# Four turned-input buffers moved to directly behind the weight ring

## The reference

```python
h = x + short_conv_mixer(rms_norm(x), w_in, conv_w, w_out)     # 1024 -> 3072 -> 1024
h = h + swiglu_ffn(rms_norm(h), w13, w2)                       # 1024 -> 2 x 2816 -> 1024
h = h + mla_mixer(rms_norm(h), ...)                            # latent attention, 8 heads
h = h + swiglu_ffn(rms_norm(h), w13, w2)
h = rms_norm(h)
h = h + concat(gla_group(...), gqa_group(...)) @ w_out         # linear attention and attention
h = h + hier_moe(rms_norm(h), ...)                             # 64 experts, 2 per token, 1024 -> 512 -> 1024
return rms_norm(h)
```

## Time and profile before

| | before |
|---|---|
| median of 3 runs | 1616.76 us |
| profiled execution: from first to last instruction | 1615.7 us |
| PE busy (share of the span) | 1312.8 us (81%) |
| DVE busy | 538.6 us (33%) |
| ACT busy | 444.6 us (28%) |
| POOL busy | 63.0 us (4%) |
| moved by DMA | 519.44 MB, mean 321 GB/s |
| chain that ended last | DMA 49%, PE 46%, DVE 2%, ACT 2% |
| mean granted TensorE clock | 0.937 |

### The profile page before, as it was taken

The page is one execution under the profiler, slowest core; times in us unless marked ns, Lnnn a source line. Parts: engine busy times, 40 slices in busy tenths (PEclk is TensorE's granted clock), DMA queues, the critical chain, the costliest instruction groups (busy, mean ns, idle before and its releaser), DMA issues.

```text
span 1615.7 us, 29952 instructions
## 1 busy us (share of the span) xinstructions
PE 1312.8 (81%) x12872; PEld 989.5 (61%) x12872; DVE 538.6 (33%) x911; ACT 444.6 (28%) x760; POOL 63.0 (4%) x84
## 2 busy tenths in 40 slices
PE   8999999999999999999676667667666766666665
PEld 8989999878999989876343343344333334333332
DVE  6665555775555568641100000001001010010001
ACT  5444343654434356621111011011011011011101
POOL 3000000002000016000000000000000000000000
PEclk9999999999999999999888898799899889898888
DMA  9555544444554535499999999999999999999997
GB/s 357 191 172 184 191 171 154 144 159 144 183 187 175 196 131 223 190 416 428 424 428 428 428 428 429 429 428 428 428 428 428 428 428 428 428 429 429 428 429 300
DMA packets 46215, 519.44 MB, mean 321 GB/s; under 512 B 5583, under 2 KB 5844, under 8 KB 8660
## 3 DMA queue, kind: packets, MB, share of 16 engines
q1 hardware_dynamic: 44928, 517.38, 78.8%
q0 software_dynamic: 896, 0.99, 0.3%
q10 hardware_dynamic: 340, 0.35, 0.1%
HBM read 517.65 MB, written 1.05 MB: 321 GB/s over the span
## 4 chain that ended last, share of the span: by engine, by line
DMA 49%; PE 46%; DVE 2%; ACT 2%; issue 1%; SPq 0%; POOL 0%; ACTq 0%; POOLq 0%; DVEq 0%
DMA work<-in_moe_units 48%; PE ps L298 12%; PE ps L300 12%; PE ps L299 12%; PE ps L2233 5%; PE ps L2224 1%; PE ps L971 1%; PE ps L970 0%; ACT w_split L257 0%; PE ps L465 0%; DVE xT_lo L545 0%; PE ps L1672 0%; DMA work<-in_conv_w 0%; PE ps L2267 0%; PE ps L1654 0%
## 5 line engine op out<-in xcount | busy, mean ns | idle before, releaser
L2224 PE MATMUL ps<-ring,work 128*32 128x256 f32 x2976 | 203.8, 420 | 98.0 <-DMA ring<-in_moe_units 97.0
L298 PE MATMUL ps<-xT_hi,w_split 128*128 128x256 f32 x960 | 269.5, 281 | 1.4 <-DVE xT_lo L545 1.4
L299 PE MATMUL ps<-xT_lo,w_split 128*128 128x256 f32 x960 | 268.1, 279 | 0.0
L300 PE MATMUL ps<-xT_hi,w_split 128*128 128x256 f32 x960 | 267.9, 279 | 0.0
L2444 DVE TENSOR_TENSOR work<-ps,work 128x128 f32<-128x128 f32 x64 | 18.7, 292 | 745.2 <-ACT work L2358 745.2
L261 DVE TENSOR_TENSOR w_split<-ring,w_split 128x2048 fp32r<-128x2048 f32 (+3 forms) x101 | 225.4, 2234 | 96.2 <-ACT w_split L257 95.0
L257 ACT ACTIVATE w_split<-ring 128x2048 fp32r<-128x2048 f32 (+3 forms) x105 | 196.0, 1869 | 152.9 <-PE ps L300 152.9
L2224 PEld LDWEIGHTS ps<-ring,work 128*32 128x32 f32 x2976 | 95.6, 118 | 195.6 <-DMA ring<-in_moe_units 120.9
L298 PEld LDWEIGHTS ps<-xT_hi,w_split 128*128 128x128 f32 x960 | 180.2, 188 | 3.4 <-issue 2.2
L299 PEld LDWEIGHTS ps<-xT_lo,w_split 128*128 128x128 f32 x960 | 179.8, 187 | 1.0
L300 PEld LDWEIGHTS ps<-xT_hi,w_split 128*128 128x128 f32 x960 | 180.3, 188 | 0.0
(11 more groups left out here) (364 smaller groups left out, 1620.8 us busy)
## 6 DMA issues: line engine op xcount, KB each, us to landing
ring<-in_moe_units SPq DMA_DIRECT2D x124, 2048.0 KB, 27.0
ring<-in_ffn_units SPq DMA_DIRECT2D x66, 1024.0 KB, 4.8
x_slots<-in_moe_units SPq DMA_DIRECT2D x32, 2048.0 KB, 25.9
work<-in_moe_units SPq DMA_DIRECT2D x32, 2048.0 KB, 27.1
ring<-in_conv_units SPq DMA_DIRECT2D x15, 1024.0 KB, 12.0
ring<-in_win_units SPq DMA_DIRECT2D x9, 1024.0 KB, 5.0
ring<-in_wo_units SPq DMA_DIRECT2D x4, 1024.0 KB, 5.8
ring<-in_wout_units SPq DMA_DIRECT2D x4, 1024.0 KB, 4.8
```

What stands on the lines that cost most here:

```text
L298: pe.matmul(out_ap, stat_hi, mov_hi, start=first, stop=False, skip_group_check=True)
L299: pe.matmul(out_ap, stat_hi, mov_lo, start=False, stop=False, skip_group_check=True)
L300: return pe.matmul(out_ap, stat_lo, mov_hi, start=False, stop=last, skip_group_check=True)
L2224: last = pe.matmul(ps[CAP * j:CAP * j + CAP, b, 0:BLK], xstat[:, 4 * half + k, CAP * lane:CAP * lane + CAP], w[k][:, j // 2, BLK * (j % 2) ...
```

## The change

The declaration of `x_slots` moves up, from behind `h` to directly behind `ring`. Everything that names it stays as it is. The tensors `cst`, `wr`, `late_consts` (which lies over parts of these two), `pcol` and `h` are thereby placed 32,768 bytes higher, and `x_slots` lower.

```diff
         return ((U_MOE + 2) % RAW, (U_MOE + 4) % RAW, RAW + 2 * (U_WOUT % SPLIT), RAW + 2 * ((U_WOUT + 1) % SPLIT))[q]
 
+    x_slots = sb("x_slots", [P, 4, UNIT])
     cst = sb("cst", [P, NCONST])
     wr = sb("wr", [P, KD, NG + NE])
     behind = -(-(nc.lookup_mloc(cst).addr + 4 * CONST["causal"][0]) // 32) * 32
@@ -187,7 +188,6 @@
     late_consts = nc.alloc_sbuf_tensor_at("late_consts", [P, D], F32, offset=behind)
     pcol = sb("pcol", [P, NROWS])
     h = sb("h", [P, TT, D])
-    x_slots = sb("x_slots", [P, 4, UNIT])
     at = nc.lookup_mloc(x_slots).addr
     xT_hi, xT_lo, xS_hi, xS_lo = (nc.alloc_sbuf_tensor_at(name, [P, KD, T], F32R, offset=at + 4 * UNIT * q)
                                   for q, name in enumerate(("xT_hi", "xT_lo", "xS_hi", "xS_lo")))
```

## The result

The kernel with the change takes 1620.98 us (median of 13 runs, 1620.32 to 1622.15), the kernel before in the same session 1617.52 us (13 runs, 1616.63 to 1618.74). The ratio is 1.0022, 95% interval 1.0015 to 1.0030: 3.5 us slower, just past what can be told from no change. The forecast was no change, with 1614 to 1620 us as that case's own range: the time lies 1 us above this one, inside the wide range of 1612.0 to 1623.5, and in the window of the slower rival.

What follows compares the result with a forecast made beforehand. TensorE's pace was taken to bound the dense layers and weight transfers the experts; four terms of zero (0 + 0 + 0 + 0) left the median, 1616.8 us, with a range of 1612.0 to 1623.5 us.

Steps and rivals of the forecast that it cites:

- the slower rival: Dense layers' 256-column matmuls: both buffers on multiples of 128 bytes cost 1.1 to 2.2 ns each, +3.2 to +6.4 us; chance 0.10.
- Parts 1 to 3: Expert-weight loads into `x_slots`, expert matmuls reading it, VectorE and ScalarE on turned inputs: each zero; loads bounded at ±6.3 us.
- Part 4, "Against addresses": Dense split matmuls: two units with equal offsets modulo 16,384 differ in pace, so a pipeline phase fits better; zero taken.
- Part 4, "the 512-column matmuls don't care": Dense layers: similar durations, 392 ns with `zeros` and 394 with `w_split` and `xS`, so placement costs these nothing.
- Part 4, the count: Dense layers: 2,880 matmuls moving 256 columns of `xT` and 72 moving `xS`; zero, ends -12.9 and +6.4 us.
- The faster rival: Dense layers' 256-column matmuls drop to 113.3 ns at distance 0 modulo 16,384: -12.9 us, 1603.9 us; chance 0.13.
- The estimate of 109 ns: Split matmuls of 256 columns: N/2.4 + 2.5 ns from the skill's page, set against 117.7 and 113.3 in the trace.

Runs made afterwards that it cites:

- map_start: PE-only kernel on constant data: the same 48 matmuls of 256 columns at once behind 1 to 3 others; 113.3 or 117.8 ns at distances 64 and 192.
- near_192: Against the kernel before, `pcol` and `rounds_i`, then `x_slots`, stand directly behind the ring, distance 192 modulo 256: 1604.64 us, ratio 0.9921.
- parted: As near_192, but the turned inputs are parted: `xS` directly behind the ring at distance 0, `xT` at 192: 1611.73 us, ratio 0.9968 against before.
- map_pace: PE-only kernel, one source line for each matmul kind and distance; moving 256 input columns: 120.0, 117.8, 118.7, 113.3 ns at 0, 64, 128, 192.
- map_fine: PE-only kernel with the kinds of map_pace, distances in 16-byte steps, and both operands shifted together; group means from 114.2 to 120.0 ns between multiples of 64.

## Why the prediction failed where it did

The forecast of no change, on the ground that addresses don't set the pace, missed by 3.5 us against before. That the time still lies in the wide range is owed to the slower rival's window, which that range took in whole and which was given 0.10, and in part to luck: of the kinds of matmul that it left out or gave no cost at either end, one cost 2.1 us and the 512-column ones gave 4.1 back.

**Parts 1 to 3**, transfers into `x_slots`, expert matmuls, VectorE and ScalarE: zero was right. The period of the experts is 29.36 us, L808 takes 693 ns, the writes of ScalarE and VectorE into the turned inputs take as long as before, to within 0.15 us in the sum of every group, and the dense matmuls account for 4.4 of the shift of 4.5 us at the end of their stage.

**Part 4, "Against addresses"**, is the step that failed. The observation was sound: U_MLA+4 and U_MLA+8 had the same distance and different paces, and map_start shows that two paces at one distance can come from what ran before; for these two units themselves that isn't shown. What the prediction drew from it was not sound. "A phase fits better than a collision" treats the two as exclusive; the distance decides which phases exist, and at distance 0 neither 113.3 nor 117.8 does. The two paces at one address said nothing of what another address would bring.

**Part 4, "the 512-column matmuls don't care"**, failed too, and by the way it was read. It compared durations, and a pace of 0.26 us from a group of four with a slow first one, too coarse for a difference of 6.6 ns. The starts within one feed-forward unit give 233.3 ns, a number that the argument never looked at and that the `zeros` rows can't vouch for. It was worth -4.1 us (762 matmuls).

**Part 4, the count.** The 336 matmuls with `w_split` moving 256 columns past `xT` were not in the sum at all. They were at 113.8 ns and had the most to lose: +2.1 us.

**The slower rival** came true in its size for the term that it named: the 2,952 matmuls that move 256 columns of the inputs cost 6.11 + 0.31 = 6.4 us, its upper end. That the total is 3.5 and not 6.4 us comes from the two terms that it lacked, +2.1 and -4.1, and from scatter in the experts. Its mechanism, both buffers on multiples of 128, was half right: distance 0 stays at 120.0 when both are shifted off such a multiple, so it is the distance that counts; and at a distance of 128 the pace is mostly 118.4 to 118.9, while among the multiples of 64 only those of 256 have 120.0 every time.

**The faster rival** had nearly the right price for its term and the wrong place. 1616.8 - 12.9 was written for distance 0 modulo 16,384. near_192, at 192 modulo 256, has -11.6 us for the 2,880 matmuls; that the whole kernel gives -12.9 too is chance, since that has the other kinds and some waits in it.

By the Trainium skill, page "TensorE: Matmul & The Clock Gate", section "Step-by-step: what each phase is for", the moving stream and the weight loads come through two independent read ports. The traces don't bear out what I drew from it, that placement can't matter: the same instructions take 113.7 ns in near_192 and 119.9 in after, and only declarations have moved between these two. The estimate of 109 ns was misapplied besides: the page's section "Back-to-back issue gap" gives that formula for an isolated matmul, and says that in a stream of weight loads and matmuls both set the spacing. No split matmul of 256 columns here holds 109 ns; 113.3 is the least that held over a group.

**The chances.** 0.13 for slower, 0.10 of it for this rival, was too little. Two paces of one instruction, unexplained, with addresses a candidate named in the text, on 2,900 instructions that bound half the kernel, is a reason to spread, not to settle at 0.74 for no change.

## What to carry to other kernels

If PE bounds a stage with back-to-back matmuls of this kind, the distance between the moving and the stationary buffer modulo 256 bytes is a parameter to tune: here it is worth 0.8% of the whole kernel, for the order of a few declarations, and a PE-only kernel with one source line for each distance shows in one run which paces there are. Which of two paces the whole kernel then gets it can't tell: parted had the same distance as near_192 for its largest kind and lost 7 us by what ran ahead. Read such costs from start to start, kind by kind, and count every kind; opposite signs can hide each other. And when one instruction has two paces in a trace, that rules out no cause: test what sets the choices and what chooses as two questions.

## What the runs showed of the hardware

All at a granted clock of 1.00, 2.4 GHz. At distances that are multiples of 64 bytes, split matmuls of 128 stationary columns and 256 moving ones, back to back, have steady paces of 113.3, 117.8 or 120.0 ns (272, 282.7 and 288 periods of 2.4 GHz, worked out), and 118.4 to 120.0 at distance 128; those of 512 columns, 226.7 to 233.4. Of these distances 0 modulo 256 is the slowest for 256 columns and the fastest for 512. At 64 and 192 two paces exist for 256 columns, 4.45 ns apart; what ran ahead chooses, the choice then held over 288 matmuls in a row (parted, first stage), and repeated unchanged each time. A matmul of 64, 128 or 192 columns among these costs 0.11 us, nearly as much as one of 256.

Open: what in the chip gives the period of 256 bytes; why 64 and 192 have two states; and by what rule the run ahead chooses one. The distances between multiples of 64 were seen once or twice for each kind and in no whole kernel; chan at 32 had 117.8 ns in map_pace and 116.7 in map_fine.
